# Nine Strassen pairs instead of five in the second unit of the last down projection, with the four extra pairs' hidden forms made during the first unit

## The reference, cut to what matters

```python
def _swiglu(h, w_gate, w_up, w_down):
    return (jax.nn.silu(h @ w_gate) * (h @ w_up)) @ w_down      # 2048 -> 5632 -> 2048
...
x = x + _swiglu(_rmsnorm(x, ffn_norm[i]), ffn_w_gate[i], ffn_w_up[i], ffn_w_down[i])
```

## Time and profile before

| | |
|---|---|
| median of 3 runs | 2071.18 us (2071.16 to 2071.28) |
| the profiled execution | 2071.52 us, with a span of 2069.9 us |
| granted TensorE clock | 1.00 over the whole span |
| PE busy | 2062.3 us, 100% |
| DVE busy | 1698.5 us, 82% |
| ACT busy | 1177.7 us, 57% |
| unit 0 of the last down projection | about 1833.0 to 1950.1 us of the span |
| unit 1 | about 1950.1 to 2066.5 us |

### The profile page before, as it was taken

How to read it: one execution, slowest core, us unless ns; L and a number is a source line. 1 busy time by engine, 2 the same in 40 slices (tenths; PEclk the granted TensorE clock), 3 DMA queues, 4 the chain that set the end, 5 groups by cost and what they waited for, 6 DMA issues and landing times.

```text
span 2069.9 us, 27700 instructions
## 1 busy us (share of the span) xinstructions
PE 2062.3 (100%) x9421; PEld 1712.9 (83%) x9421; DVE 1698.5 (82%) x1933; ACT 1177.7 (57%) x1487; POOL 105.7 (5%) x128
## 2 busy tenths in 40 slices
PE   9999999999999999999999999999999999999999
PEld 8888888888888888888888888888888888888887
DVE  6777668999999987867798787579999999978766
ACT  6548656556655654545555554566656565654453
POOL 0000000100010000000000000000000000000000
PEclk9999999999999999999999999999999999999999
DMA  8564456777777776767666766567777777767674
GB/s 276 166 196 150 141 166 203 231 230 224 227 223 234 217 230 199 222 201 210 205 206 203 215 200 201 175 200 221 225 231 218 234 228 229 216 219 215 199 219 147
DMA packets 226722, 432.10 MB, mean 209 GB/s; under 512 B 14432, under 2 KB 21232, under 8 KB 226640
## 3 DMA queue, kind: packets, MB, share of 16 engines
q1 hardware_dynamic: 209328, 399.23, 58.8%
q0 software_dynamic: 17168, 31.75, 8.9%
q10 hardware_dynamic: 144, 0.03, 0.0%
HBM read 428.86 MB, written 2.10 MB: 208 GB/s over the span
## 4 chain that ended last, share of the span: by engine, by line
PE 97%; DVE 2%; ACT 1%; issue 1%; ACTq 0%; DVEq 0%
PE ps L733 24%; PE ps L735 24%; PE ps L734 24%; PE ps L589 3%; PE ps L522 3%; PE ps L524 3%; PE ps L523 3%; PE ps L590 3%; PE ps L591 3%; PE ps L538 2%; PE ps L695 1%; PE ps L693 1%; PE ps L694 1%; PE ps L648 1%; DVE w_lo L1356 0%
## 5 line engine op out<-in xcount | busy, mean ns | idle before, releaser
L1356 DVE TENSOR_TENSOR w_lo<-stage,w_hi 128x1024 fp32r<-128x1024 f32 x688 | 830.3, 1221 | 224.9 <-ACT w_hi L962 221.3
L962 ACT ACTIVATE w_hi<-stage 128x1024 fp32r<-128x1024 f32 x688 | 709.8, 1054 | 490.8 <-PE ps L735 365.6
L733 PE MATMUL ps<-w_hi,xs 128*128 128x512 f32 x1122 | 439.4, 392 | 0.3
L735 PE MATMUL ps<-w_hi,xs 128*128 128x512 f32 x1122 | 437.0, 389 | 0.0
L734 PE MATMUL ps<-w_lo,xs 128*128 128x512 f32 x1122 | 436.6, 389 | 0.0
L733 PEld LDWEIGHTS ps<-w_hi,xs 128*128 128x128 f32 x1122 | 210.7, 188 | 44.2 <-DVE gated L1637 1.1
L735 PEld LDWEIGHTS ps<-w_hi,xs 128*128 128x128 f32 x1122 | 210.6, 188 | 44.1
L734 PEld LDWEIGHTS ps<-w_lo,xs 128*128 128x128 f32 x1122 | 210.7, 188 | 42.9
L733 PE MATMUL ps<-w_hi,hs 128*128 128x512 f32 x584 | 227.6, 390 | 0.0
L735 PE MATMUL ps<-w_hi,hs 128*128 128x512 f32 x584 | 227.2, 389 | 0.0
L734 PE MATMUL ps<-w_lo,hs 128*128 128x512 f32 x584 | 227.2, 389 | 0.0
(11 more groups left out here) (217 smaller groups left out, 3041.2 us busy)
## 6 DMA issues: line engine op xcount, KB each, us to landing
stage<-in_w_gate SPq DMA_DIRECT2D x176, 512.0 KB, 4.0
stage<-in_w_up SPq DMA_DIRECT2D x176, 512.0 KB, 5.0
stage<-in_w_down SPq DMA_DIRECT2D x176, 512.0 KB, 5.0
stage<-in_conv_w_in SPq DMA_DIRECT2D x96, 512.0 KB, 4.9
stage<-in_attn_w_in SPq DMA_DIRECT2D x48, 512.0 KB, 4.4
stage<-in_w_gate POOLq DMA_DIRECT2D x86, 256.0 KB, 5.7
stage<-in_attn_w_out SPq DMA_DIRECT2D x32, 512.0 KB, 4.6
stage<-in_conv_w_out SPq DMA_DIRECT2D x32, 512.0 KB, 4.3
```

Of the source, the lines that this page charges most:

```text
L733: pe.matmul(ps[:, bank, :], hi, b_hi, start=start, stop=False)
L735: return pe.matmul(ps[:, bank, :], lo, b_hi, start=False, stop=stop)
L962: nc.scalar.activation(w_hi[:, j % RING, :], stage[:, at, :], ACT.Copy).then_inc(hi_done, 1)
L1356: tt(w_lo[:, p, :], stage[:, stage_at(first + j), :], f32(w_hi[:, p, :]), ALU.subtract).then_inc(lo_done, 1)
```

## The change

In the last layer unit 1 mixes nine pairs, 6, 7, 9, 10, 12, 13, 15, 16 and 18; unit 0 keeps five. The forms of the four more pairs (7, 10, 13, 16) are made in unit 0 as well, at slots 22, 28, 34 and 38, so that unit 0 now makes nine forms. Their places in `hs` are free only when unit 0's plain slots of that pair are used, hence the new waits on `slot_used`. The other layer is unchanged, apart from where its forms lie in the wider `sh`.

```diff
-        sh = xs[:, KT // 2:, :].rearrange("p k (b t) -> p (k b) t", b=2)
+        sh = xs[:, :, :].rearrange("p k (b t) -> p (k b) t", b=2)
...
-        DN_PAIRS = (6, 9, 12, 15, 18)
+        DN_PAIRS = (((6, 9, 12, 15, 18),) * 2, ((6, 9, 12, 15, 18), (6, 7, 9, 10, 12, 13, 15, 16, 18)))
+        DN_FORMS = ({6: 7, 9: 13, 12: 19, 15: 25, 18: 31}, {6: 7, 9: 13, 12: 19, 7: 22, 15: 25, 10: 28, 18: 31, 13: 34, 16: 38})
-        FORM_SLOTS = (7, 13, 19, 25, 31)
...
-                        if kp not in DN_PAIRS:
+                        if kp not in DN_PAIRS[layer][u]:
                             plain_slot(n, j, kp, side, FT // 2, hs, bank_free,
                                        half_made if u and layer and j == FT - 1 else None)
                         elif side == 0:
-                            if u == 0:
-                                pe.wait_ge(mixed_hidden_ready, DN_MIXED * layer + DN_PAIRS.index(kp) + 1)
-                            mixed_pair(n, kp, DN_PAIRS, LAYER_MIXED * layer + ALL_FFN_MIXED + DN_MIXED * u, hs,
-                                       hidden_mixed, bank_free)
+                            if kp not in DN_PAIRS[layer][0] or u == 0:
+                                pe.wait_ge(mixed_hidden_ready, forms_made(layer, form_of(layer, kp) + 1))
+                            mixed_pair(n, kp, DN_PAIRS[layer][u], down_mixed(layer, u), hs,
+                                       lambda kp, s, form: hidden_mixed(layer, kp, form), bank_free)
...
-            def hidden_forms_high(layer, s):
-
-                act.wait_ge(slot_used, S_DN1 if layer else S_DN0)
-                act.wait_ge(hidden_step, 4 * (DN_MIXED * layer + s) + 4)
-                nc.scalar.activation(sh[:, 3 * s:3 * s + 3, 0:P], mixed_hidden[:, 0:3, :],
+            def hidden_forms_high(layer, kp):
+
+                s = form_of(layer, kp)
+                at = form_place(layer, s)
+                first = S_DN1 if layer else S_DN0
+                act.wait_ge(slot_used, first if kp in DN_PAIRS[layer][0] else first + 2 * kp + 2)
+                act.wait_ge(hidden_step, 4 * forms_made(layer, s) + 4)
+                nc.scalar.activation(sh[:, at:at + 3, 0:P], mixed_hidden[:, 0:3, :],
...
-                forms = {at: [lambda s=s: hidden_forms_high(layer, s)] for s, at in enumerate(FORM_SLOTS)}
+                forms = {at: [lambda kp=kp: hidden_forms_high(layer, kp)] for kp, at in DN_FORMS[layer].items()}
...
+                if kp not in DN_PAIRS[layer][0]:
+                    dve.wait_ge(slot_used, (S_DN1 if layer else S_DN0) + 2 * kp + 2)
...
-                forms = merged({at: [lambda s=s: mix_hidden(layer, s)] for s, at in enumerate(FORM_SLOTS)},
-                               {at + 1: [lambda s=s: mixed_hidden_low(layer, s)] for s, at in enumerate(FORM_SLOTS)})
+                forms = merged({at: [lambda kp=kp: mix_hidden(layer, kp)] for kp, at in DN_FORMS[layer].items()},
+                               {at + 1: [lambda kp=kp: mixed_hidden_low(layer, kp)] for kp, at in DN_FORMS[layer].items()})
```

More of the change, by code:

```diff
@@ L394, in trunk @@
         CONV_MIXED = sum(map(len, CONV_PAIRS))
-        FFN_MIXED, DN_MIXED = len(MIXED_PAIRS), len(DN_PAIRS)
+        FFN_MIXED = len(MIXED_PAIRS)
+        DN_MIXED = tuple(sum(map(len, pairs)) for pairs in DN_PAIRS)
         ALL_FFN_MIXED = (BLOCKS - 1) * FFN_MIXED + len(LAST_MIXED)
-        LAYER_MIXED = ALL_FFN_MIXED + 2 * DN_MIXED + CONV_MIXED
+        LAYER_MIXED = ALL_FFN_MIXED + DN_MIXED[0] + CONV_MIXED
         def mixed_of(i):
@@ L410, in conv_evicts, with down_mixed, forms_made, form_of @@
             return EVICTS * (BLOCKS + i) + 2 * DOWN_EVICTS
+        def down_mixed(layer, u):
+            return LAYER_MIXED * layer + ALL_FFN_MIXED + sum(map(len, DN_PAIRS[layer][:u]))
+        def forms_made(layer, s):
+            return len(DN_FORMS[0]) * layer + s
+        def form_of(layer, kp):
+            return list(DN_FORMS[layer]).index(kp)
+        def form_place(layer, s):
+            return 3 * s + (0 if layer else KT)
         def conv_mixed(i):
-            return ALL_FFN_MIXED + 2 * DN_MIXED + sum(map(len, CONV_PAIRS[:i]))
+            return ALL_FFN_MIXED + DN_MIXED[0] + sum(map(len, CONV_PAIRS[:i]))
         block = ctx.enter_context(nc.Block())
@@ L746, in x_mixed_last, with hidden_mixed @@
                 return moved_forms[:, form, 0:P], moved_forms[:, form, P:TOK]
-            def hidden_mixed(kp, s, form):
+            def hidden_mixed(layer, kp, form):
                 if form == 3:
                     return half(hs, 2 * kp, 1)
-                return sh[:, 3 * s + form, 0:P], sh[:, 3 * s + form, P:TOK]
+                at = form_place(layer, form_of(layer, kp)) + form
+                return sh[:, at, 0:P], sh[:, at, P:TOK]
             def half_slot(slot, kk):
@@ L1249, in ffn @@
                 return merged(unit_steps(last), {6: [lambda: hidden_high(BLOCKS * layer + last, last)]})
-            def hidden_forms_high(layer, s):
-                act.wait_ge(slot_used, S_DN1 if layer else S_DN0)
-                act.wait_ge(hidden_step, 4 * (DN_MIXED * layer + s) + 4)
-                nc.scalar.activation(sh[:, 3 * s:3 * s + 3, 0:P], mixed_hidden[:, 0:3, :],
+            def hidden_forms_high(layer, kp):
[5 more added lines that the diff above has]
+                nc.scalar.activation(sh[:, at:at + 3, 0:P], mixed_hidden[:, 0:3, :],
                                      ACT.Copy).then_inc(mixed_hidden_hi, 1)
-                nc.scalar.activation(hs[:, 2 * DN_PAIRS[s], P:TOK], mixed_hidden[:, 3, :],
+                nc.scalar.activation(hs[:, 2 * kp, P:TOK], mixed_hidden[:, 3, :],
                                      ACT.Copy).then_inc(mixed_hidden_hi, 1)
             def down(layer, first, before):
-                def count(u):
-                    return LAYER_MIXED * layer + ALL_FFN_MIXED + DN_MIXED * u
+                pairs = DN_PAIRS[layer]
                 def take(u):
-                    return lambda: take_p1(LAYER_UNITS * layer + BLOCKS + u, first + FT * u, DN_PAIRS, count(u))
-                forms = {at: [lambda s=s: hidden_forms_high(layer, s)] for s, at in enumerate(FORM_SLOTS)}
-                unit_slots(first, FT, DN_PAIRS, count(0), merged(before, forms, {TAKE_SLOT: [take(0)]}))
-                unit_slots(first + FT, FT, DN_PAIRS, count(1),
+                    return lambda: take_p1(LAYER_UNITS * layer + BLOCKS + u, first + FT * u, pairs[u], down_mixed(layer, u))
+                forms = {at: [lambda kp=kp: hidden_forms_high(layer, kp)] for kp, at in DN_FORMS[layer].items()}
+                unit_slots(first, FT, pairs[0], down_mixed(layer, 0), merged(before, forms, {TAKE_SLOT: [take(0)]}))
+                unit_slots(first + FT, FT, pairs[1], down_mixed(layer, 1),
                            merged({TAKE_SLOT: [take(1)]}, {} if layer else two_norm_steps(0)))
@@ L1724, in ffn, with mix_hidden @@
                 return merged(unit_steps(last), {6: [lambda: hidden_low(done + last, last)]})
-            def mix_hidden(layer, s):
-                done = DN_MIXED * layer + s
-                k1 = 2 * DN_PAIRS[s]
+            def mix_hidden(layer, kp):
+                done = forms_made(layer, form_of(layer, kp))
+                k1 = 2 * kp
                 dve.wait_ge(hid_turned, BLOCKS * (layer + 1))
@@ L1742, in mix_hidden, with mixed_hidden_low @@
                 tt(mixed_hidden[:, 3, :], a21, a11, ALU.subtract).then_inc(hidden_step, 1)
[L1744 to L1748, removed]
+            def mixed_hidden_low(layer, kp):
+                s = form_of(layer, kp)
+                k1 = 2 * kp
+                at = form_place(layer, s)
+                if kp not in DN_PAIRS[layer][0]:
+                    dve.wait_ge(slot_used, (S_DN1 if layer else S_DN0) + 2 * kp + 2)
+                dve.wait_ge(mixed_hidden_hi, 2 * forms_made(layer, s) + 2)
+                tt(sh[:, at:at + 3, P:TOK], mixed_hidden[:, 0:3, :], f32(sh[:, at:at + 3, 0:P]), ALU.subtract)
                 tt(hs[:, k1, TOK + P:], mixed_hidden[:, 3, :], f32(hs[:, k1, P:TOK]),
@@ L1752, in down @@
             def down(layer, first, before):
-                done = LAYER_MIXED * layer + ALL_FFN_MIXED
+                pairs = DN_PAIRS[layer]
                 part_done = out_ready if layer else res_added
@@ L1761, in take @@
                         dve.wait_ge(res_squared, 4 + 8 + 4)
-                    take_mixed(LAYER_UNITS * layer + BLOCKS + u, done + DN_MIXED * (u + 1), down_evicts(layer, u))
+                    take_mixed(LAYER_UNITS * layer + BLOCKS + u, down_mixed(layer, u + 1), down_evicts(layer, u))
                 def add_rows(u):
@@ L1784, in norm @@
                     return {5: [lambda: res_low(2, j, FFN_TURN)], 7: [lambda: res_low(2, j + 1, FFN_TURN)]}
-                forms = merged({at: [lambda s=s: mix_hidden(layer, s)] for s, at in enumerate(FORM_SLOTS)},
-                               {at + 1: [lambda s=s: mixed_hidden_low(layer, s)] for s, at in enumerate(FORM_SLOTS)})
```

(10 more changed lines are left out.)

## The result

The changed kernel takes 2075.93 us (median of 13 runs, 2075.68 to 2076.43), against 2071.18 us before (13 runs, 2070.68 to 2071.44): 4.75 us more, a ratio of 1.0023 (95% interval 1.0016 to 1.0031). The profiled execution took 2076.17 us, with a span of 2074.4. Its mean granted clock is 0.999, as in each of the other 12, where the profiled execution before had 1.000.

A forecast was written before the change was run, and what follows sets the result against it. PE's matmul count times 0.2268 us bounds the kernel while DVE delivers low parts in time. Lateness of 7.7 us at slot 39 less 2.72 gives +5.0: 2076.2 us for the median, range 2075.0 to 2078.3.

The forecast's parts named there:

- The gain of 2.72 us: Unit 1: four pairs take 21 matmuls instead of 24, so 12 x 0.2268 = 2.72 us less on PE.
- 4.33 us for each form, 1.80 of it idle: Unit 0: each form costs DVE 4.33 us, 1.80 of it idle before the next split, waiting on ACT's fixed order.
- DVE's way from slot 22 to slot 39: Unit 0: DVE, through slot 22 at 1888.75, has slot 39's low part at 1943.96; PE would start that slot at 1936.5.
- The restart: After a PE wait: 0.14 us from DVE's end to the matmul, 0.08 more until the pace is even.
- PE's waits, 2.3, 3.1 and 1.6 us: Unit 0: PE waits for low parts at slots 26, 32 and 39, some 7.5 us in all.
- The rival of the clock: TensorE's clock falls in the waits, after the 3.1 us one; 2 us taken as lost, 2078; chance 0.07.
- the prediction's last sentence: Wrong if idle times are shorter at the new forms, PE also waits in unit 1, or granted clock is under 1.00.
- No cost in unit 1: Unit 1, three pairs: DVE needs 13.8 us against PE's 15.0, so PE has no waits there.
- The additions: Rival: additions come late in unit 1, DVE waits in each of four patterns, 2 to 4 us, 2079; chance 0.07.
- A covered round trip: Rival: the 1.80 us vanish at each form in unit 0, PE never waits, 2068.5; chance 0.05, partly covered 0.09.

The follow-up runs named there:

- the forms alone: The change with nine forms made in unit 0 but unit 1 keeping its five old mixed pairs: 2078.96 us, ratio 1.0036.
- all forms one slot later: The change with every form's high parts on ACT and low parts on DVE one slot later in the last layer: 2068.5 us, ratio 0.9987.
- the kernel before with the same edit: The kernel before, its five forms' high and low parts one slot later in the last layer: 2071.31 us, ratio 1.0000.
- six pairs: The change with only pair 7 of the four new pairs, form at slot 22: 2074.53 us, run again on another chip 2073.24 us.
- seven pairs: The change with only pairs 7 and 10 of the new ones, forms at slots 22 and 28: 2077.18 us, ratio 1.0026.
- the filled one of seven: The seven-pair version plus eight zero-operand matmuls ahead of slot 26 and twelve ahead of slot 32 of unit 0: 2075.16 us, ratio 1.0019.

## Why the prediction was right, point by point

It said 2076.2, in a range of 2075.0 to 2078.3; measured are 2075.93. Three steps held closely, one was off without a cost, and one rival was half right. That the fall of the clock cost nothing is luck: the prediction counts on a full clock throughout.

- **The gain of 2.72 us:** 7.7 with the forms alone against 4.75 with the whole change leaves 2.9 for the 12 matmuls, and 2.8 are left where the forms cost nothing. In the timelines of PE unit 1 takes 113.33 us from its first matmul to its last (1957.47 to 2070.80), against 116.06 before (1950.18 to 2066.24): 2.73 less.
- **4.33 us for each form, 1.80 of it idle:** 4.34 and 1.80 at the new form shown above. That the idle time is a real cost is shown by the version with all forms one slot later, and that it is one only where DVE is behind by the kernel before with the same edit.
- **DVE's way from slot 22 to slot 39:** by the prediction 1888.75 to 1943.96, 55.2 us; here from 1888.48 to 1943.67, the same 55.2 us. All of this execution lies 0.27 us earlier than that of before, as the form at slot 19 does, and slot 39 started at 1936.58 before, so it starts 1943.72 + 0.27 - 1936.58 = 7.4 us late, where I had 7.6. The restart took 0.05 us and not 0.14.
- **PE's waits, 2.3, 3.1 and 1.6 us:** 2.17, 1.44 and 1.26 were measured, 4.9 in all and not some 7.5. A row counts its idle time from the modelled end of the matmul before, which lies 0.16 us behind the next start of an even pace. From start to start PE loses 2.33, 1.60 and 1.42 us, and these are the figures to compare. The second is wrong, and why is in the rows of PE: behind the first wait matmuls start 0.43 us apart until 1908.35, about twice 0.2268. From 1904.65 to slot 32 PE needs 1.7 us more than 69 matmuls at the even pace, and this comes out of the wait at slot 32. With these 1.7 the three make 7.1 of the 7.4 us above. The end does not notice, since PE goes on at slot 32 when DVE has its low part.
- **The rival of the clock** was right that the clock falls in such a wait, and wrong that 2 us must come of it. By the prediction's last sentence a clock under 1.00 would have shown it wrong; it was 0.66 in the window from 1905 to 1910, and the time came out all the same, because DVE was late again. The prediction had not reasoned this out. I had put it behind the wait of 3.1 us at slot 32; the fall came behind 2.2 us at slot 26, with DVE late again afterwards. Where nothing is late behind the wait it does cost about that: 1.4 us between the medians of the groups of the six pairs (1.6 between the two traces), and 1.9 between those of the seven, there without a trace of the slower kind.
- **No cost in unit 1:** right. DVE is busy 13.98 of 15 us in the dense windows and PE never idle. The additions did not come late here: the DMA share is up to 0.87, but no wait of DVE on a DMA is in the list for unit 1. The rival has something in it all the same. In the profiled executions with six and seven pairs, all but the filled one of seven, DVE waits once in unit 1 for a DMA into `stage`, for 0.23 to 2.12 us, and PE is not held up by it.
- **A covered round trip** was named as the rival on the other side, at 2068.5. It is not what the change did, but the edit that makes it so gives 2068.5.

## What to carry to other kernels

Before moving work under another engine's cover, add up that engine's idle times around such work as well as its busy time, and follow both engines slot by slot until they meet: 2.5 us of work were 4.3 us of time here. Idle time that comes from two engines of fixed order waiting for each other is free while there is a lead, and is paid in full once the lead is used up; putting the answer one step later in both queues removed it and turned +4.75 us into -2.8. A wait inside a stretch that another engine paces can hide a second loss, so a smaller dose of a change may cost more (2077.18 us with seven pairs, 2075.93 with nine).

## What the runs showed of the hardware

- **A wait of about 2.2 us of TensorE can lower its clock, in some executions and not in others.** Behind it six or seven matmuls start 0.43 us apart instead of 0.23, the pace of the lower of its two levels (1.2 for 2.4 GHz), with a granted clock of 0.66 to 0.69 in the window of 5 us around them, and then the pace is the old one. With six pairs 11 of 22 executions show it by a mean clock of 0.999, eight of one set of eleven and three of the other. Waits of 0.45, 1.29, 1.44 and 1.26 us had no slow matmul behind them in the profiled executions. Filling the wait with matmuls on a zero operand left a mean clock of 1.000 in all 22 executions of the two versions tried; so it is the idleness, as far as another chip may be compared. One of the 15 executions of the kernel before beside two of these versions also has 0.999, at 2072.91 us; no trace of it was kept, and what lowered its clock is open. The Trainium skill (TensorE: Matmul & The Clock Gate, Part 1) says that the throttled clock is the default and that activity releases it, and that the number of slow matmuls at the start of one kernel varies from run to run. These runs show such a variation behind a wait in mid-kernel, in 8 and 3 of 11 executions.
- **Where a tile lies in SBUF can set the pace of matmuls that read it.** With `hs` and `sx` 64 bytes further on, 128x512 matmuls reading `hs` started 0.233 us apart in place of 0.2268, and the whole kernel took 26 us more. With the filling in place and nothing moved (its zero operand 8 columns wide instead of 16) the cost was gone. The groups show it for both tiles (mean of the high-part matmuls 396 for 391 ns on `hs`, 397 for 392 on `sx`), and not for `xs`. Other distances were not tried.
